# A hybrid encoder trunk: two gate tiles of the second merge computed in the recurrence's last round, and merges with another tile order, an in-place mix and smaller row pieces

## The reference

```python
h = rmsnorm(x, norm1_g)
u, v, q, i, z_f, z_b, g_o, g_a, g_b = split_cols(h @ w_in)      # nine blocks of 1024 columns
ya = gmlp_branch(gelu(u), gelu(v), ...)                          # chunked spatial gating
yb = hgrn2_branch(q, i, z_f, z_b, lbs, onorm_g, g_o)             # gated recurrence, 8 heads, two directions
m = sigmoid(g_a) * (ya @ w_branch_a) + sigmoid(g_b) * (yb @ w_branch_b)   # the two merges
x = x + m @ w_out
x = x + expert_choice_ffn(rmsnorm(x, norm2_g), ...)              # 16 experts
return rmsnorm(x, final_g)
```

## Time and profile before

| | us |
|---|---|
| median of three runs | 2656.83 |
| the profiled execution, whole | 2653.25 |
| its span, first to last instruction | 2651.5 |
| TensorE busy in it | 2417.7 (91%) |
| VectorE, ScalarE, GpSimd busy | 1259.5, 1025.7, 401.7 |

### The profile page before, as it was taken

One profiled execution on the slowest core, in us unless ns is written; L12 is line 12 of the kernel. 1 busy time (PEld: TensorE's weight loads), 2 busy tenths in 40 slices (PEclk: granted clock), 3 DMA queues, 4 the chain that ended last, 5 costly groups with the idle time before them and its releaser, 6 DMA issues. The chain is left out here.

```text
span 2651.5 us, 58648 instructions
## 1 busy us (share of the span) xinstructions
PE 2417.7 (91%) x25099; PEld 2236.5 (84%) x25099; DVE 1259.5 (48%) x1660; ACT 1025.7 (39%) x1474; POOL 401.7 (15%) x270
## 2 busy tenths in 40 slices
PE   4999899999999999999967997992999999999993
PEld 4999899999999998998957997882888888888882
DVE  4123320006457457457553111336677667766663
ACT  4222221113332333333322111222667666666763
POOL 1221131111111101101103110002212112121110
PEclk7999999999999999999988999995999999999996
DMA  3112241111101101101005222823787878878774
GB/s 119 30 31 79 86 127 51 51 60 34 43 18 44 35 26 44 35 26 44 27 2 159 71 91 93 278 104 139 254 308 275 309 279 312 306 273 303 286 266 177
DMA packets 185947, 351.04 MB, mean 132 GB/s; under 512 B 10816, under 2 KB 113216, under 8 KB 185792
## 3 DMA queue, kind: packets, MB, share of 16 engines
q1 hardware_dynamic: 179648, 327.78, 35.0%
q0 software_dynamic: 6144, 20.98, 3.1%
HBM read 301.54 MB, written 47.19 MB: 132 GB/s over the span
## 5 line engine op out<-in xcount | busy, mean ns | idle before, releaser
L1714 DVE TENSOR_TENSOR ex_w_lo<-ex_raw,ex_w_hi 128x1024 fp32r<-128x1024 f32 x256 | 306.2, 1223 | 135.1 <-ACT ex_w_hi L1706 132.0
L1706 ACT ACTIVATE ex_w_hi<-ex_raw 128x1024 fp32r<-128x1024 f32 x256 | 265.7, 1058 | 59.2 <-PE ex_out L1948 51.7
L176 PE MATMUL hg_proj<-trunk_h_hi,hg_w_hi 128*128 128x320 f32 x768 | 248.0, 323 | 15.4 <-issue 15.4
L177 PE MATMUL hg_proj<-trunk_h_lo,hg_w_hi 128*128 128x320 f32 x768 | 240.8, 314 | 1.0 <-issue 1.0
L178 PE MATMUL hg_proj<-trunk_h_hi,hg_w_lo 128*128 128x320 f32 x768 | 240.2, 313 | 0.0
L1946 PE MATMUL ex_out<-ex_w_hi,ex_x_hi 128*128 128x512 f32 x512 | 205.3, 401 | 2.2 <-DVE ex_x_lo L1732 2.2
L1947 PE MATMUL ex_out<-ex_w_hi,ex_x_lo 128*128 128x512 f32 x512 | 200.1, 391 | 0.0
L1948 PE MATMUL ex_out<-ex_w_lo,ex_x_hi 128*128 128x512 f32 x512 | 200.0, 391 | 0.0
L176 PE MATMUL hg_proj<-trunk_h_hi,trunk_w_hi 128*128 128x320 f32 x512 | 161.9, 316 | 5.3 <-POOLq L201 5.3
L1706 ACT ACTIVATE ex_w_hi<-all_raw 128x1024 fp32r<-128x1024 f32 x128 | 133.1, 1056 | 79.2 <-PE ex_out L1948 66.8
L176 PEld LDWEIGHTS hg_proj<-trunk_h_hi,hg_w_hi 128*128 128x128 f32 x768 | 147.1, 191 | 18.8 <-issue 16.8
(11 more groups left out here) (326 smaller groups left out, 6157.7 us busy)
## 6 DMA issues: line engine op xcount, KB each, us to landing
all_raw<-in_w_exp_gate_dram SPq DMA_DIRECT2D x32, 2048.0 KB, 11.9
ex_raw<-in_w_exp_up_dram SPq DMA_DIRECT2D x32, 2048.0 KB, 10.3
ex_raw<-in_w_exp_down_dram SPq DMA_DIRECT2D x32, 2048.0 KB, 18.0
trunk_w_raw<-in_w_in_dram SPq DMA_DIRECT2D x48, 512.0 KB, 4.1
hg_w_raw<-in_w_in_dram SPq DMA_DIRECT2D x16, 512.0 KB, 4.4
ya<-gm_ya SPq DMA_DIRECT2D x8, 640.0 KB, 3.5
m_a<-ma_m SPq DMA_DIRECT2D x8, 640.0 KB, 3.5
yb<-hg_Kt_b SPq DMA_DIRECT2D x8, 640.0 KB, 4.9
```

The source lines that it names most:

```text
L176: nc.tensor.matmul(out, self.hi[s][:, k, :], x_hi[:, k, c], start=(k == 0), stop=False)
L177: nc.tensor.matmul(out, self.hi[s][:, k, :], x_lo[:, k, c], start=False, stop=False)
L1706: nc.scalar.activation(w_hi[u % RING][:], src, ACT.Copy).then_inc(s["w_hi_ready"], 1)
L1714: ops.tensor_tensor(w_lo[u % RING][:], src, w_hi[u % RING][:].bitcast(F32), ALU.subtract).then_inc(s["w_lo_ready"], 1)
```

## The change

The recurrence's last round now has three tiles: its own, and the gate tiles of columns 0 and 1 of mb. Their sigmoids go to two buffers `C.sg` that the trunk holds from its start on; the recurrence uses the same two as `q` and `vT`. The tile after them (gate 2, mb's first) is prepared in the shared buffers (`hand_hi`, `hand_lo`). In `merge` the tiles have an explicit order, unrolled: ma goes G0 G1 B0 G2 B1 G3 ... G7 B6 B7 (G is a gate tile, B a branch tile), mb goes G2 B0 G3 B1 G4 B2 G5 B3 G6 B4 G7 B5 B6 B7. There are three `sg` buffers by turns; the branch is multiplied in place into them and stored from there, so a gate of column r waits for the store of column r - 3. y comes in 32 pieces of 128 x 320 columns through a ring of five (the quarters of `m_prev` and a spare); VectorE makes every low part, GpSimd only splits weights. The gate groups of tile 0 are read out after pieces 8, 15, 22 and 29, and the first branch tile's groups wait for their own 8 pieces each. Two weight tiles are loaded ahead of the first row piece, where there was one.

```diff
+    def hand_hi(self, nc, act, r, t):
+        rs, n = self.raw_slot[t], self.per * r
+        turn = self.raw_slot.count(rs) * r + self.raw_slot[:t + 1].count(rs)
+        act.wait_ge(self.group_done, PARTS * (n + 1 + CREDIT))
+        act.wait_ge(self.loaded[rs], 16 * turn)
+        nc.scalar.activation(self.hi[0][:], self.raw[rs][:], ACT.Copy).then_inc(self.hi_ready, 1)
+    def hand_lo(self, nc, pool, r, t):
+        pool.wait_ge(self.hi_ready, self.per * r + t + 1 + CREDIT)
+        nc.gpsimd.tensor_tensor(self.lo[0][:], self.raw[self.raw_slot[t]][:], self.hi[0][:].bitcast(F32),
+                                ALU.subtract).then_inc(self.lo_ready, 1)
...
-        tiles_before, tiles_last = tiles_with(-1)[1:], [(HEADS - 1, TGO)]
+        tiles_before, tiles_last = tiles_with(-1)[1:], [(HEADS - 1, TGO)] + [(HEADS, t) for t in range(AHEAD)]
...
+            if type(r) is int and r == HEADS:
+                nc.scalar.activation(C.sg[t][:, c], out, ACT.Sigmoid).then_inc(free, 1)
...
-                W.load(sp, HEADS, 0, next_tile)
+                W.load(sp, HEADS, 0, gates_ahead[0])
                 store(sp, HEADS - 2)
+                W.load(sp, HEADS, 1, gates_ahead[1])
+                W.load(sp, HEADS, AHEAD, next_tile)
                 store(sp, HEADS - 1)
...
+    PER, LEAD = 2, 1 if ahead else 2
+    order = [(True, ahead + i) for i in range(LEAD)]
+    for b in range(KC):
+        order.append((False, b))
+        if ahead + LEAD + b < KC:
+            order.append((True, ahead + LEAD + b))
...
-        rows = RowSplit(st, y_dram, [a[:, i * T // 2:(i + 1) * T // 2] for a in (m, m_prev) for i in range(2)], 2, y_hi, y_lo)
+        rows = RowSplit(st, y_dram, [m_prev[:, i * PART:(i + 1) * PART] for i in range(PARTS)] + [spare[:]], PARTS, y_hi, y_lo)
...
+        def act_gate(act, n, part):
+            r = order[n][1]
+            if part == 0 and r >= len(sg):
+                act.wait_ge(m_stored[r % len(sg)], 16 * (r // len(sg)))
+            out, free = W.result(act, *tile(n), part)
+            nc.scalar.activation(sg[r % len(sg)][:, part * PART:(part + 1) * PART], out, ACT.Sigmoid).then_inc(free, 1)
...
+                nc.vector.tensor_tensor(mix[:, c], out, mix[:, c], ALU.mult).then_inc(free, 1)
...
             def _(sp):
-                W.load(sp, 0, BRANCH, cols(w_branch, 0))
+                sp_tile(sp, 1)
+                sp_tile(sp, 2)
                 rows.load(sp)
+                sp_tile(sp, 3)
                 rows.ready(sp)
                 sp_prev(sp, 0)
+                for n in range(1, len(order)):
+                    if n > 1:
+                        sp_tile(sp, n + 2)
+                    gate, b = order[n]
+                    if not gate:
+                        sp_tail(sp, b)
+                        sp_prev(sp, b + 1)
...
-                gate_after = {len(rows.pieces) * (part + 1) // PARTS - 2: part for part in range(PARTS)}
+                gate_after = {7 * g + 8: g for g in range(PARTS)}
                 for i in range(len(rows.pieces)):
                     rows.split_hi(nc, act, i)
-                    if i == 1:
-                        W.split_hi(nc, act, 0, BRANCH)
+                    if i == 3:
+                        act_split(act, 1)
                     if i in gate_after:
                         act_gate(act, 0, gate_after[i])
...
-                rows.split_lo(dve, nc.vector, 1, rows.lo_odd)
+                for i in range(len(rows.pieces)):
+                    rows.split_lo(dve, nc.vector, i % 2, (rows.lo_even, rows.lo_odd)[i % 2], i, i + 1)
```

More of the change, by code:

```diff
@@ L681, in pool_round @@
         def pool_round(pool, tiles):
-            for tile in tiles:
-                W.split_lo(nc, pool, *following(*tile))
+            for i, tile in enumerate(tiles):
+                if tiles is tiles_last and i == len(tiles) - 1:
+                    W.hand_lo(nc, pool, *following(*tile))
+                else:
+                    W.split_lo(nc, pool, *following(*tile))
         def k_level(eng, ops, g, j):
@@ L1153, in sp_tail, with source, sp_tile @@
+        def source(n):
+            gate, r = order[n]
+            return cols(w_in, col_gate + r * P) if gate else cols(w_branch, r * P)
+        def sp_tile(sp, n):
+            if n < len(order):
+                W.load(sp, *tile(n), source(n))
+            elif n == len(order) and next_tile is not None:
+                W.load(sp, *tile(n), next_tile)
+        def sp_tail(sp, b):
             if adds:
-                sp.wait_ge(s["added"], PARTS * (r + 1) + PARTS * CREDIT)
+                sp.wait_ge(s["added"], PARTS * (b + 1))
@@ L1169, in act_round @@
[L1169 to L1181, removed]
+                W.moved(sp, *tile(branch_at[b]))
@@ new lines, in sp_tail, with sp_prev, act_split @@
+            sp.dma_start(m_out[b * P:(b + 1) * P, :], sg[b % len(sg)][:]).then_inc(m_stored[b % len(sg)], 16)
+        def sp_prev(sp, b):
+            if adds and b < KC:
+                if b:
+                    sp.wait_ge(s["added"], PARTS * b)
+                sp.dma_start(m_prev[:], m_in[b * P:(b + 1) * P, :]).then_inc(s["m_prev_loaded"], 16)
+        def act_split(act, n):
+            if n < len(order) or n == len(order) and next_tile is not None:
+                W.split_hi(nc, act, *tile(n))
@@ new lines, in pool_split @@
+        def pool_split(pool, n):
+            if n < len(order) or n == len(order) and next_tile is not None:
+                W.split_lo(nc, pool, *tile(n))
+        def act_gate(act, n, part):
[4 more added lines that the diff above has]
+            nc.scalar.activation(sg[r % len(sg)][:, part * PART:(part + 1) * PART], out, ACT.Sigmoid).then_inc(free, 1)
@@ L1182, in dve_round, with dve_branch @@
+        def dve_branch(dve, b):
+            n = branch_at[b]
+            r, t = tile(n)
+            mix = sg[b % len(sg)]
+            if b >= ahead:
+                W.moved(dve, *tile(order.index((True, b))))
+            if adds:
+                dve.wait_ge(s["m_prev_loaded"], 16 * (b + 1))
             for part in range(PARTS):
                 c = slice(part * PART, (part + 1) * PART)
-                out, free = W.result(dve, r, BRANCH, part)
-                nc.vector.tensor_tensor(m[:, c], out, sg[:, c], ALU.mult).then_inc(free, 1)
+                out, free = W.result(dve, r, t, part)
+                nc.vector.tensor_tensor(mix[:, c], out, mix[:, c], ALU.mult).then_inc(free, 1)
@@ L1228, in _ @@
                 W.pool_credit(pool)
[L1229 to L1236, removed]
+                for n in range(1, len(order) + 1):
+                    pool_split(pool, n)
             @block.tensor
@@ L1240, in _ @@
                 W.pe_credit(pe)
-                def pe_round(r, first):
+                for n, (gate, r) in enumerate(order):
                     for part in range(PARTS):
[L1244 to L1253, removed]
+                        if not gate and r == 0:
+                            rows.ready(pe, KC * (part + 1))
+                        W.multiply(nc, pe, *tile(n), part, *((h_hi, h_lo) if gate else (y_hi, y_lo)))
             @block.vector
             def _(dve):
-                dve.sem_inc(s["added"], PARTS * CREDIT)
-                rows.split_lo(dve, nc.vector, 1, rows.lo_odd)
+                for i in range(len(rows.pieces)):
+                    rows.split_lo(dve, nc.vector, i % 2, (rows.lo_even, rows.lo_odd)[i % 2], i, i + 1)
                 rows.ready(dve)
-                with dve.Fori(0, KC) as r:
-                    dve_round(dve, r)
+                for b in range(KC):
+                    dve_branch(dve, b)
 def residual_route(nc, C, x_prompt, x_sample, w_out, m_dram, norm2_g, w_router, x3, h2, w_first):
```

77 lines of the change are left out of this document (35 added, 42 removed).

## The result

The changed kernel takes 2652.62 us, the kernel before 2659.40, medians of 16 runs each side by side: a ratio of 0.9973, interval 0.9965 to 0.9981. It is faster, by 7 us where I had forecast 14, and lies outside my range by 0.6 us. Three later comparisons of the same kernel gave 0.9961 [0.9948, 0.9974], 0.9976 [0.9966, 0.9987] and 0.9979 [0.9969, 0.9988].

The account below looks back on a forecast made before the run. TensorE, busy 2417.7 of 2651.5 us, was taken as the bound, with holes at the merges' starts and in the last round. Terms 6.5 - 28.2 + 4.0 + 3.4 + 0.5 gave -13.8 us; forecast 2641 us, range 2630 to 2652.

Parts of the forecast that it names:

- Term 1: Recurrence's last round: with eight more groups, OUT ends later, as in the round before; +6.5 us.
- Term 2: mb's stretch without holes: two gate tiles fewer at 14.08 us each; -28.2 us.
- Term 3: Start of both merges: y in small pieces, a ring turn of 4.0 us, rows ending at 32.0 instead of 28.0 us.
- Term 3a: mb's start: m_prev's load waits for the last piece, so B0's end moves with the rows' end; +4.0 us.
- Term 3b: ma's start: moves with the last reading of tile 0's gate groups, second gate tile in front buys nothing; +3.4 us.
- Term 4: mb's steady part: no stall for stores, short waits for m_prev at two places; +0.5 us.
- At nothing: Items priced at zero: mix in place, VectorE's subtractions beside the landing, and unrolled loops in the merges.
- B: Rival at the merges' starts: turn shortens only to 4.8 us; 2651 us, no measurable change; chance 0.13.
- A: Rival at the merges' starts: rows come quicker, a turn of 3.6 us; 2632 us; chance 0.22.
- C: Rival at the merges' starts: turn stays at 6.4 us, deciding from 5.15 on; 2670 us; chance 0.06.
- D: Rival in the last round: added work hides nothing, round grows by the whole 28.2 us; 2663 us; chance 0.02.

Follow-up runs that it names:

- no_gates_ahead: Changed kernel with the two gate tiles taken out of the recurrence's last round, mb running all 16 tiles; 1.0024 of the kernel before.
- unrolled_1: Kernel before with the rounds of both merges written out instead of in hardware loops, first of two traces; 1.0003 of the kernel before.
- gates_early: Changed kernel with tile 0's gate groups read after pieces 4, 10, 16 and 22; 0.9975 of the kernel before.
- lead1: Changed kernel with one gate tile ahead of ma's first branch tile instead of two; 0.9970 of the kernel before.

## Why the prediction was wrong

The direction was right, and each term had the right sign and place. The terms' sizes came out short all on one side, one stretch that I had put at no change grew, and the base was a lucky trace. Of the 11.6 us between 2641 and 2652.6, 4.6 is the base: I had set 2654.8 for the kernel before, between its profiled execution and the first three runs, and 16 runs put it at 2659.4. The other 7 is the gain itself.

- **Term 1, the last round:** +6.5 forecast; 6.4 in the pair of windows, +7.0 on the means of four. Right. The round before was the right template.
- **Term 2, two tiles fewer:** -28.2 is their time without a hole, and right as arithmetic. The kernel before, like the changed one, had one gate tile ahead of B0, so the cover that no_gates_ahead shows was not lost against it.
- **Term 3, the rows:** 32.0 us forecast for the rows' end; 32.0 in ma and 32.2 in mb, last reading at 30.4 forecast, 30.7 and 30.4 measured. The first piece landed 6.4 us after ma's start and the 31st at 30.3, so a turn was 4.0 us, as forecast. The landing had a median of 2.6 to 2.8 us in the four traces, where I had taken 2.8. The Trainium skill's fit ("DMA: Bandwidth & Descriptors", "Anatomy of one DMA") is for transfers issued from GpSimd; the 2.4 us that I worked out from it is an estimate, and the median of these loads by SyncE lies above it in all four traces.
- **Term 3a, mb's start:** +4.0 forecast, +4.1 in the pair, +4.9 on the means. The rows ended 29.1 us after mb's start in the mean before and 32.8 after. TensorE's waits in mb's first two tiles grew from 6.7 us to 11.9 on the means. Of these the wait for m_prev, which I had booked as unchanged, grew from 0.6 to 1.4 us in the four traces before to 2.6 to 3.4 after. **Term 3b, ma:** +3.4 forecast, +5.1 in the pair, +4.3 on the means, with the caution that the same tiles, unchanged, took up to 54.6 us in unrolled_1; the last three groups before B0 ran partly at half clock in two of the four traces of the changed kernel. The last reading came at 26.2 to 27.0 us before and 29.8 to 30.7 after, as the term said. My reason for it (the reading of tile 0's groups) was half the truth: gates_early moved that reading, and ma didn't follow.
- **Term 4, new waits in mb's steady part:** the stores cost nothing, as forecast. For m_prev I gave +0.5; the 12 tiles took 170.6 us, where 12 x 14.08 is 169.0, with one wait of 1.2 us at B6. The mean of the four is -26.3 against -28.2, so +1.9. Its loads landed at a median of 5.2 us instead of 4.8. Mis-sized.

On the means, terms 1, 3 and 4 were short by 0.5, 1.8 and 1.4, together 3.7, which makes -10.1 of the forecast -13.8. **The step that failed is the one that holds all else at nothing:** that the rest of the kernel stays as in the profiled execution. The seven rounds ahead took 4.6 us more on the means, and that is the larger part of the 8.3 us by which the traces' -5.5 falls short. Under "At nothing" I had weighed the written-out loops only where they stand, in the merges; the traces show the longer rounds in the stage behind them. How much of the 4.6 is chance and how much the written-out code, and by what way, stays open. And I treated the profiled execution as a sample of the kernel's time when it was the quickest of four.

Of the rivals, B (2651 us) is the one that the time fell nearest to, and that is luck: the turn was 4.0 us as I had it, not 4.8. A (a turn of 3.6) and C (5.15 and more) did not come, and D is refuted by the last round's 6.4. Two slips in the working changed little: 37.8 less three groups is 27.2, not 27.0, and the range began at 2630 where A's far end was 2632.

## What to carry to other kernels

Before a tile is moved out of a stage, ask what it covers where it stands, and compare with the right kernel: ahead of B0 the second gate tile costs 9 us of the new mb and not 14, because 5 us of it lie in waits. The pace of this kernel's ring was its bytes in flight over the turn: smaller pieces in a ring of fewer bytes were slower, and where the destination could take the raw data itself, the ring wasn't needed. Where a change is worth half a per cent, take several traces of the kernel before, and compare stage by stage: here a long stretch of untouched code differed by more than the change was worth. And ask what written-out code may do to the stages behind it, not only to its own.

## What was not expected of the hardware

The recurrence's seven rounds have the same instructions in all traces and took 760.4 to 772.8 us (772.8 in lead1). The half-clock stretches that reach into them add up to 20 to 51 us, and the two go together, if loosely: 760.4 with 20, 763.8 with 34, 766.3 with 34, 769.0 with 44, 772.8 with 48. Apart from one where the stage begins, the falls come at most once a round, at the loop's turn. In the kernel before one began at 822.6 us. There TensorE waits 0.7 us for ScalarE, runs ten small transposes of the values (line 557, from 819.9 us), and stands 2.4 us at the loop's turn, until 823.6:

```profile
820.00:823.00 3.00, 1.20 (x10) 0.96 (x10) 0.39 (x4) 1.76 (x2) 0.00 (x0) 0.94 0.02 5
```

The same stretch stands at each of the six turns, and after those at 1023.5 and 1224.4 us no fall came in this trace; what decides it no run here shows. VectorE's 8.15 us reciprocals, one a round, start 101.4, 102.2, 102.6, 101.9, 102.8 and 102.1 us apart in the changed kernel's first trace, where nearly every round had a fall of 6.8 us, and 99.9 to 101.8 apart in the first trace of the kernel before, where most had a fall of 3.4 us or none.
